# A seventh ring slot, memory keys written feature-major, and table and register loads moved in a decoder step

## What is computed

```python
for i in range(DEPTH):                      # memory of the prompt, both layers
    kv = rmsnorm(mem_prompt, mem_norm[i]) @ w_mem_kv[i]
    mk.append(kv[..., :XA_WIDTH].reshape(B, N_MEM, XA_HEADS, XA_DIM))
    mv.append(kv[..., XA_WIDTH:].reshape(B, N_MEM, XA_HEADS, XA_DIM))
...
h = rmsnorm(x, norm_mix[i])
mix, ns = conv_mixer(...) or retention_mixer(...)
xa = cross_attn(q_x, mem_ks[i], mem_vs[i])  # softmax(q k / 16) v
x = x + jnp.concatenate([mix, xa], axis=-1) @ w_out
x = x + hier_moe(rmsnorm(x, norm_ffn[i]), ...)
```

## Time and profile before

| | us |
|---|---|
| median of three runs | 1340.07 |
| profiled execution, its own time | 1339.78 |
| its span | 1337.9 |
| TensorE matmuls busy | 1204.8 (90%) |
| TensorE weight loads busy (beside matmuls) | 693.8 (52%) |
| VectorE busy | 355.2 (27%) |
| ScalarE busy | 153.9 (12%) |
| GpSimd busy | 11.2 (1%) |
| mean granted TensorE clock | 0.955 |
| bytes moved | 364.59 MB, 273 GB/s in the mean |

### The profile page before, as it was taken

The page is one execution under the profiler, slowest core; times in us unless marked ns, Lnnn a source line. Parts: engine busy times, 40 slices in busy tenths (PEclk is TensorE's granted clock), DMA queues, the critical chain, the costliest instruction groups (busy, mean ns, idle before and its releaser), DMA issues.

```text
span 1337.9 us, 13595 instructions
## 1 busy us (share of the span) xinstructions
PE 1204.8 (90%) x5884; PEld 693.8 (52%) x5884; DVE 355.2 (27%) x868; ACT 153.9 (12%) x340; POOL 11.2 (1%) x22
## 2 busy tenths in 40 slices
PE   6999998998998989869999999996999889888785
PEld 3467776776333434236655555563677743332233
DVE  3222213004021304223234342422300233222224
ACT  2000002002110101010201010110200021000001
POOL 0000000000000000000000000000000000000000
PEclk9999999998999999889999999998999869989998
DMA  9743338731599999994216565557954419999991
GB/s 397 302 159 126 126 128 321 313 126 63 216 430 428 421 428 428 427 427 188 79 63 238 218 227 229 216 240 303 425 188 169 176 34 430 427 428 428 428 426 75
DMA packets 27263, 364.59 MB, mean 273 GB/s; under 512 B 3152, under 2 KB 3168, under 8 KB 5056
## 3 DMA queue, kind: packets, MB, share of 16 engines
q1 hardware_dynamic: 23904, 338.99, 62.1%
q10 hardware_dynamic: 1696, 18.88, 3.4%
q0 software_dynamic: 1600, 5.81, 1.1%
HBM read 339.34 MB, written 24.32 MB: 272 GB/s over the span
## 4 chain that ended last, share of the span: by engine, by line
PE 69%; DMA 26%; DVE 2%; ACT 2%; issue 1%; POOL 0%; SPq 0%; DVEq 0%; POOLq 0%; ACTq 0%
DMA ring<-in_gu 24%; PE bank L621 21%; PE bank L429 12%; PE bank L330 8%; PE bank L486 4%; PE bank L706 4%; PE bank L476 2%; PE bank L517 2%; PE bank L316 1%; PE bank L677 1%; PE bank L442 1%; PE bank L385 1%; PE bank L787 1%; PE bank L408 1%; PE bank L768 1%
## 5 line engine op out<-in xcount | busy, mean ns | idle before, releaser
L621 PE MATMUL bank<-hT,ring 128*128 128x288 f32 x1152 | 285.7, 409 | 4.0 <-DVE hT L1077 3.3
L621 PEld LDWEIGHTS bank<-hT,ring 128*128 128x128 f32 x1152 | 218.8, 191 | 73.7 <-issue 13.9
L486 PE MATMUL bank<-ring,arena 128*32 128x512 f32 x1024 | 132.7, 656 | 55.0 <-DMA ring<-in_gu 53.3
L429 PE MATMUL bank<-arena,ring 128*128 128x288 f32 x640 | 155.7, 406 | 1.8 <-DVEq L1141 1.8
L429 PEld LDWEIGHTS bank<-arena,ring 128*128 128x128 f32 x640 | 121.4, 190 | 35.6 <-issue 2.2
L330 PE MATMUL bank<-ring,arena 128*128 128x512 f32 x256 | 111.2, 594 | 3.1 <-DVE arena L1077 3.1
L486 PEld LDWEIGHTS bank<-ring,arena 128*32 128x32 f32 x1024 | 32.5, 115 | 146.8 <-DMA ring<-in_gu 80.2
L476 PE MATMUL bank<-arena 128*128 128x512 f32 (+1 forms) x192 | 102.0, 659 | 2.4 <-DVE arena L1207 1.7
L330 PEld LDWEIGHTS bank<-ring,arena 128*128 128x128 f32 x256 | 48.2, 190 | 63.4 <-issue 61.9
L517 PE MATMUL bank<-arena 128*128 128x288 f32 x256 | 71.4, 427 | 2.1 <-issue 1.7
L476 PEld LDWEIGHTS bank<-arena 128*128 128x128 f32 (+1 forms) x192 | 32.9, 198 | 73.9 <-issue 72.4
(11 more groups left out here) (206 smaller groups left out, 806.1 us busy)
## 6 DMA issues: line engine op xcount, KB each, us to landing
ring<-in_gu SPq DMA_DIRECT2D x64, 2048.0 KB, 24.9
ring<-in_dn SPq DMA_DIRECT2D x32, 2048.0 KB, 17.4
ring<-in_rin SPq DMA_DIRECT2D x14, 2048.0 KB, 13.4
ring<-in_wkv SPq DMA_DIRECT2D x8, 2048.0 KB, 17.4
ring<-in_cin SPq DMA_DIRECT2D x8, 2048.0 KB, 8.7
ring<-in_kc SPq DMA_DIRECT2D x8, 2048.0 KB, 8.6
ring<-in_vc SPq DMA_DIRECT2D x8, 2048.0 KB, 14.0
ring<-in_st SPq DMA_DIRECT2D x8, 2048.0 KB, 14.9
```

Source lines behind the costliest of these rows:

```text
L429: mm = pe.matmul(bank[1 + o % 4][:, 0:T], w[:, k, :], cat[:, k, :], start=(k == 0), stop=(k == kt - 1))
L486: mm = pe.matmul(bank[2][32 * e:32 * e + 32, :], xt[:, k, 32 * e:32 * e + 32], wv[:, e, kk, :], start=(k == 0), stop=(k == KD - 1), skip_g ...
L621: mm = pe.matmul(outs[o], w[:, o, k, :], src[:, k, :], start=(k == 0), stop=(k == KD - 1))
```

## The change

- `R` goes from 6 to 7. The further passes keep six slots (`SPILL`). The room comes from the descriptor scratch, given as 2,048 bytes of each partition in place of the default, and from the arena, 576 words shorter: `th` and `nrm` (`ms`, `rstd`) move into regions of other stages.
- Key pieces (c < 2) of `memory_kv` are computed with the weight as the stationary side, 128 features x 256 tokens in each half of a bank; ACT copies the banks straight to `KT`, and the key outputs are stored from `KT` and put in order on the host side. `turn_keys`, `keys_turned`, `Ktok`, `keys1` and their waits go. ACT's wait for the store of the layer-0 keys moves from before the first query copy to before layer 1's key copies; VectorE's wait for the store of layer 1's keys goes.
- `squares` issues an activation `Sqrt` of one element before the squares; after the square root of the norms `ffn0` and `ffn1`, and at the start of `attention`, stands an `Exp` of one element.
- TensorE, ACT and VectorE load `npass` before the last pack, GpSimd before its wait for the last pack. The branches stay where they were.

```diff
-R = 6
+R = 7
+SPILL = 6
...
-KEYS_IN = {1: (0, 1), 3: (2, 3)}
...
-        arena = sb("arena", 21568)
+        arena = sb("arena", 20992)
...
-        th = [ar(MSO + 288 * i, T) for i in range(2)]
+        th = [ar(SQO + 1184 + 288 * i, T) for i in range(2)]
...
-        nrm = ar(MSO, 576)
+        idle = small[0:1, 62:63]
+        nrm = ar(PHO + 2752, 576)
...
@@ TensorE, memory_kv
+                if c < 2:
+                    for o in range(2):
+                        f = (2 * mb + o) * P
+                        for k in range(KD):
+                            if i == 0 and j == 0 and o == 0:
+                                pe.wait_ge(S("normed"), k + 1)
+                            mm = pe.matmul(bank[KV_BANKS[i][j]][:, o * NM:(o + 1) * NM], w[:, k, f:f + P],
+                                           src[:, k, :], start=(k == 0), stop=(k == KD - 1), skip_group_check=True)
+                    mm.then_inc(S("kv_sum"), 1)
+                    return
...
@@ TensorE, experts; the same two lines on ACT and VectorE
                 for i in range(PACKS):
+                    if i == PACKS - 1:
+                        pe.wait_ge(S(f"npass{L}"), 1)
+                        more = pe.value_load(npass[0:1, L:L + 1], min_val=0, max_val=PASSES - 1)
...
-                    if L == 0 and i in KEYS_IN:
-                        pe.wait_ge(S("gt_out"), i)
-                        turn_keys(1, KEYS_IN[i])
-                        pe.wait_ge(S("kt_out_a"), 2 + KEYS_IN[i][1] + 1)
...
-            pe.wait_ge(S("ktok_out"), 4)
-            turn_keys(0, range(4))
-
-            pe.wait_ge(S("kt_out_a"), 2)
-            pe.wait_ge(S("kt_out_d"), 2)
+            pe.wait_ge(S("kt_out"), 4)
             pe.wait_ge(S("v_out"), 4)
...
@@ ACT, squares
+                act.activation(idle, C("eps")[0:1, :], ACT.Sqrt)
                 for k in range(KD):
...
                 act.activation(ms[:, 0:n], bank[7][:, 0:n], ACT.Sqrt, scale=1.0 / D, bias=C("eps")) \
                    .then_inc(S("ms_out"), 1)
+                if name in ("ffn0", "ffn1"):
+                    act.activation(idle, C("eps")[0:1, :], ACT.Exp)
...
@@ ACT, keys_ahead
+                act.wait_ge(S("keys_stored0"), 16)
                 for j in range(4):
                     act.wait_ge(S("kv_sum"), 8 + j + 1)
-                    act.activation(keys1[:, j % 2, (j // 2) * 512:(j // 2 + 1) * 512],
-                                   bank[(4, 7, 0, 1)[j]][:, :], ACT.Copy).then_inc(S("kv1_out"), 1)
+                    act.activation(KT[:, 2 * j:2 * j + 2, :], v3(bank[(4, 7, 0, 1)[j]][:, :], 2), ACT.Copy) \
+                       .then_inc(S("kv1_out"), 1)
...
@@ ACT, attention
                 act.wait_ge(S("normed"), NORM_DONE[f"mix{i}"])
+                act.activation(idle, C("eps")[0:1, :], ACT.Exp)
...
-            dve.wait_ge(S("keys_stored1"), 16)
...
-    nc = bacc.Bacc("TRN2", target_bir_lowering=False, num_devices=1)
+    nc = bacc.Bacc("TRN2", target_bir_lowering=False, num_devices=1, dynamic_dma_scratch_size=2048)
```

More of the change, by code:

```diff
@@ L289, in spill @@
                             sp.wait_ge(S(f"spill_dve{L}"), p * (STEP_DVE * PACKS) + i * STEP_DVE + SPILL_DVE["began"])
-                            for j in range(R):
+                            for j in range(SPILL):
                                 src = a["gu"][bass.ds(i * 4 + (L * 4 * PACKS + j), 1)] if j < 4 else \
@@ L332, in memory_kv @@
                 mm.then_inc(S("kv_sum"), 1)
[L334 to L341, removed]
             def attention(i):
@@ L857, in memory_kv @@
                     act.wait_ge(S("kv_sum"), j + 1)
-                    act.activation(Ktok[:, j % 2, (j // 2) * 512:(j // 2 + 1) * 512], bank[j][:, :], ACT.Copy) \
-                       .then_inc(S("ktok_out"), 1)
-                for g in (1, 3):
-                    act.wait_ge(S("kt_turned"), g + 1)
-                    act.activation(KT[:, 2 * g:2 * g + 2, :], v3(bank[g][:, :], 2), ACT.Copy) \
-                       .then_inc(S("kt_out_a"), 1)
+                    act.activation(KT[:, 2 * j:2 * j + 2, :], v3(bank[j][:, :], 2), ACT.Copy).then_inc(S("kt_out"), 1)
             def keys_ahead():
+                act.wait_ge(S("keys_stored0"), 16)
                 for j in range(4):
                     act.wait_ge(S("kv_sum"), 8 + j + 1)
-                    act.activation(keys1[:, j % 2, (j // 2) * 512:(j // 2 + 1) * 512],
-                                   bank[(4, 7, 0, 1)[j]][:, :], ACT.Copy).then_inc(S("kv1_out"), 1)
+                    act.activation(KT[:, 2 * j:2 * j + 2, :], v3(bank[(4, 7, 0, 1)[j]][:, :], 2), ACT.Copy) \
+                       .then_inc(S("kv1_out"), 1)
                 act.wait_ge(S("kv1_out"), 4)
-                act.dma_start(a["out_mk"][1].rearrange("(m p) n -> p m n", p=P), keys1) \
+                act.dma_start(a["out_mk"][1], KT) \
                     .then_inc(S("keys_stored1"), 16)
@@ L894, in store_state @@
                     .then_inc(S(f"state_stored{f}"), 16)
-            def keys_turned(groups):
-                for g in groups:
-                    act.wait_ge(S("kt_turned"), 4 + g + 1)
-                    act.activation(KT[:, 2 * g:2 * g + 2, :], v3(bank[(4, 7)[g % 2]][:, :], 2), ACT.Copy) \
-                       .then_inc(S("kt_out_a"), 1)
             def attention(i):
                 act.wait_ge(S("normed"), NORM_DONE[f"mix{i}"])
+                act.activation(idle, C("eps")[0:1, :], ACT.Exp)
                 for j in range(9):
@@ L954, in experts @@
                 for i in range(PACKS):
+                    if i == PACKS - 1:
+                        act.wait_ge(S(f"npass{L}"), 1)
+                        more = act.value_load(npass[0:1, L:L + 1], min_val=0, max_val=PASSES - 1)
                     act.wait_ge(S("gu_sum"), 4 * PACKS * L + 4 * i + 4)
@@ L960, in experts @@
                         values_ahead(VALUES_IN[i])
-                    if L == 0 and i in KEYS_IN:
-                        keys_turned(KEYS_IN[i])
                     act.wait_ge(S("gt_turned"), PACKS * L + i + 1)
@@ L1085, in memory_kv @@
                        .then_inc(S("v_out"), 1)
-                for g in (0, 2):
-                    dve.wait_ge(S("kt_turned"), g + 1)
-                    dve.tensor_copy(KT[:, 2 * g:2 * g + 2, :], v3(bank[g][:, :], 2)).then_inc(S("kt_out_d"), 1)
             def attention(i, xo):
@@ L1255, in experts @@
                 for i in range(PACKS):
+                    if i == PACKS - 1:
+                        dve.wait_ge(S(f"npass{L}"), 1)
+                        more = dve.value_load(npass[0:1, L:L + 1], min_val=0, max_val=PASSES - 1)
                     dve.wait_ge(S("tanh"), PACKS * L + i + 1)
@@ L1476, in store_memory @@
             def store_memory():
-                pool.wait_ge(S("ktok_out"), 4)
-                pool.dma_start(a["out_mk"][0].rearrange("(m p) n -> p m n", p=P), Ktok).then_inc(S("keys_stored0"), 16)
+                pool.wait_ge(S("kt_out"), 4)
+                pool.dma_start(a["out_mk"][0], KT).then_inc(S("keys_stored0"), 16)
                 pool.wait_ge(S("v_out"), 4)
```

22 lines of the change are left out of this document (5 added, 17 removed).

## The result

The changed kernel takes 1307.41 us (median of four runs, 1302.5 to 1309.8), the kernel before 1340.12 on the same chip (1339.09 to 1340.31): ratio 0.975, 95% interval 0.972 to 0.978. That is 32.7 us less, and 21.6 were forecast; the direction was right, the size lies outside the range. The profiled execution took 1305.89 us with a span of 1304.1, 33.8 under the span before.

A forecast was written before the change was run, and what follows sets the result against it. The prediction took TensorE to set the end, except where it waits for the ring, a quarter of the span. Its terms summed to 21.6 us, taken from the profiled 1339.78 to give 1318.2 us; range 1311 to 1327.

The forecast's parts named there:

- the pass count: Branch after the experts, both layers: loading earlier removes 0.7 us ahead of each branch, 1.4 in all, not the branch itself.
- memory keys: Layer 0: key matmuls write the keys turned, so the projection begins 1.6 us earlier; in layer 1 nothing.
- the square roots: Routing norms of both layers: ACT's table load for the square root leaves the chain, 1.3 us each, 2.6 in all.
- the first softmax: First attention: the exponential begins 1.3 us earlier, plus 0.7 for a dip of TensorE's clock that may go, 2.0 us.
- the routing exponentials: Routing of layer 1: the early table load gains 0.65 us, limited by the ranks, whose last matmul ended at 1081.22.
- seventh slot, two expert stages: Each expert stage has one slot fewer to fetch, as pack 1's first is fetched early: 4.9 us each, 9.8 in all.
- seventh slot, second attention: Second attention: keys 3 are issued together with keys 2, beside the same store, so it ends 3.85 us earlier.
- The small activation at the start: Ahead of the memory's squares, for which TensorE waits: the added one-element activation costs 0.3 us.
- Rival (5): Slower: weight loads of the memory key matmuls don't hide, 48.6 us at the full 190 ns, giving 1366.8 us; chance 0.03.
- Rival (1): The clock falls out otherwise: layer 1's picking matmuls get 4.5 us back after earlier exponentials, giving 1313.7 us; chance 0.20.
- rival (4): Concerns the table loads; its statement and size are cut from the text given; chance 0.03.
- GpSimd's scratch: GpSimd's transfers with the smaller descriptor scratch: cost taken as 0, at most 3.0 us if the second close transfer must wait.

## Why the prediction was wrong

The range failed at one step: **the pass count**, "Loading earlier removes the 0.8 ahead of the branch, not the branch", and in the list of what would show it, "the branch is as long as before". The first half holds as far as it goes (0.73 and 0.41 us against 0.7 each). The second treats 6.12 and 3.63 us as the price of a branch, when it is the price of that branch at that place in TensorE's program. The part called memory keys moved it by 192 instructions, and both branches became short, with a granted clock of 1.00 in place of 0.75 in the norm sum behind the first: 12.0 us, by the kernel before with 192 idle instructions, where nothing else was changed. No rival had it. One row shown ahead of the prediction spoke of it: the same instruction with 6122 and 3626 ns, with nothing in the computation to explain the difference. The prediction set no lower bound to the branch. Had it let both fall to a third of a microsecond, for which no row gave the number, the low end of the range, 1311, would have gone down by another 9 us and held the result. The result without the 12.0 us would be 1319.4, near the forecast, and that nearness is partly luck: the square roots were taken 2.4 us too high and the first softmax 1.0, the routing exponentials 0.9 too low, and the totals carry a microsecond or two that no term has.

Term by term:

| term | forecast | runs |
|---|---|---|
| seventh slot, two expert stages | 9.8 | 5.4 + 4.5 = 9.9 |
| seventh slot, second attention | 3.85 | 3.9 |
| memory keys, with the small activation ahead of them | 1.3 | 1.6 |
| first softmax | 2.0 | 1.0 |
| square roots of two norms | 2.6 | 0.17 |
| routing exponentials, layer 1 | 0.65 | 1.6 |
| loads of the pass count | 1.4 | 1.1 |
| length of the branches | 0 | 12.0 |
| sum | 21.6 | 31.3 |

The sum of the right column is 1.4 us short of the 32.7 measured, well within what single runs differ by.

*The seventh slot* came out as worked, in size and in its signs (pack 1 fetched ahead, one wait in the attention, 4.9 us a slot). What looked like a surplus of 3.2 us in stage 0 of the kernel after is mostly luck of the profile of before. Its windows (columns as the earlier trace rows):

```profile
358.00:362.00 4.00, 3.91 (x24) 1.34 (x28) 0.00 (x0) 0.00 (x0) 0.00 (x0) 0.57 0.26 103
576.00:584.00 8.00, 7.46 (x30) 3.71 (x23) 2.59 (x6) 0.38 (x1) 0.00 (x0) 0.57 1.00 426
...
1078.00:1082.00 4.00, 3.22 (x18) 3.08 (x17) 2.00 (x11) 1.62 (x12) 0.00 (x0) 0.56 0.00 0
```

The first two lie in stage 0 at a granted clock of 0.57, and all seven other kernels with six slots are 2.5 to 3.4 us faster there. Stage 1 goes by its picking matmuls as well, which are drawn by the run. Kernels with seven slots gain 8.0 and 8.6 us there with picks of 7.9 and 8.0 us, and 3.3 to 5.7, the kernel after among them, with picks of 10.5; those with six gain 2.8 to 4.5 with fast picks and -2.5 to 0 with slow ones.

*Memory keys*: no transposes and no second copy, and the size as worked. The sum of the second norm stands ahead of layer 0's last key and value matmuls; first the kernel before, then the kernel after:

```profile
45.63 1.13 PE L316 MATMUL bank<-arena,cst 128*128 128x288 f32 x4
...
45.23 1.13 PE L315 MATMUL bank<-arena,cst 128*128 128x288 f32 x4
```

From there to the projection (76.67 and 74.66) it is 31.0 us in all seven kernels with the old keys and 29.4 in all seven with the new ones: 1.6. The other 0.4 of the 2.01 in the table came ahead of it and are luck: by the run, the clock moves that point by up to 4 us in kernels of either kind (44.98 to 49.10 us in those without idle instructions at the head; granted clock over 17 to 25 us 1.00 in both kernels shown here, 0.57 with the loads alone, at 49.05). The small activation at the start, priced at 0.3, costs at most 0.2: TensorE's first matmul begins at 9.22 to 9.33 us with it, and at 9.10 to 9.29 without. Rival (5), weight loads that don't hide, is refuted by the 218 ns.

*Square roots.* The step "1.3 each" took a load that ended at 304.47 as standing alone between the sum and the root. The sum of squares ended only at 303.12 + 1.24 = 304.36 in that profile, so the load was hidden but for 0.1 us: 0.08 and 0.09 measured. The row of the matmuls beside the load wasn't read:

```profile
303.12 1.24 PE L316 MATMUL bank<-arena,cst 128*128 128x288 f32 x4 [0.99 <-DVE arena L1066]
```

The stretch with the first of these norms is 1.66 us longer in the kernel after. All 13 other profiles are longer there than the one of before, by 0.03 to 1.66, with and without the small activations, so this is no cost of them.

*First softmax*: 1.03 for the load, and the 1.7 us of slow clock go or stay by the run, not by the load: they are missing in kernels without the small activations as well (granted clock over 205 to 230 us: 0.93 before, 1.00 in all 13 other profiles).

*Routing exponentials*: the cap "their last matmul ended at 1081.22" took the ranks' time as fixed. Before, at a granted clock of 0.56 (the third window above), they took 1.47 us; in the kernel after they took 0.83, at 0.96:

```profile
1054.00:1057.00 3.00, 2.19 (x18) 2.08 (x18) 2.46 (x13) 0.00 (x0) 0.00 (x0) 0.96 0.00 0
```

That part is not the tables' alone. Of the six kernels with the small activations three have ranks of 0.83 us, at a granted clock of 1.00 while they run, and gain 2.0 us from the second output projection to the picks; the other three have ranks of 1.41 to 1.47 us, at 0.50 to 0.53, and gain 1.2. The eight without them have -0.4 to 0.8. The difference of the means is 1.7, of which the norm's load is 0.1. Rival (1) expected the picks behind the ranks to profit too. In the kernel after they took 10.54 us, at a granted clock of 0.55, as before (0.56); in five other kernels they took 7.4 to 8.0, at 0.74 to 0.81, and in one 11.5, at 0.50. The three runs of before ahead of the prediction lie within 1.2 us and suggest low stretches that are the same in every run; the forecast left them so. More runs of that kernel lie between 1333 and 1345 us, with mean granted clocks of 0.951 to 0.963, so they differ by the run.

*The table loads themselves*, rival (4): no run shows a cost of a load beyond its own 1.28 us. The small activation of the kernel after starts at 578.95, 1.30 us after its load did, and takes 0.20.

*GpSimd's scratch*: no cost shows. The kernel with the ring alone, which has the small scratch, gains no less than the slots explain (17.7 us, 13.7 expected).

*Why the place matters.* The page of after lists the queue "q8 instruction" with 49 packets and 0.80 MB, 16.3 KB each. The page has 13,779 instructions, and the two instruction queues move 0.91 MB, about 66 bytes each, so one such packet holds an estimated 250 instructions: near the distance after which the lengths seem to repeat. A long branch ends right behind such a packet, and during a short one none is under way. The author's reading, which no run shows, is that a branch is long when what it jumps to lies in a packet that is still to come, and that moving it by a part of a packet changes this. That every long branch ends behind a packet is shown (12 of 12); that this packet holds the branch's target is not, since no view tells what a packet holds. The reading also fits the two lengths of before: with the ring's transfers on the engines the packet started 3.6 us after the first branch, with none beside it 1.0 us after the second. The 2.17 and 2.88 us belong to packets that had started already or started sooner; why they did is open, and no run holds the place and changes the transfers beside it.

## What to carry to other kernels

Before the length of a control instruction is taken as fixed, put idle instructions at a few distances ahead of it, in a stretch that waits anyway: here that alone was worth 13.9 us, as much as the seventh slot. The DMA view over the branch tells whether there is something to gain: a packet of an instruction queue that ends inside it, as in all 12 long ones here. A part is credited with what its stretch shows and not with the difference of two totals, since a change in one place moves the code, and the clock, in others: the memory keys, worth 1.6 us, came with a total some 17 us lower. Where a load or a wait is to be hidden, look for the other work that ends at the same time: it sets what is left to gain, and its own time may move too.

## What was not expected of the hardware

- The same COMPARE_BRANCH over the same skipped code takes 0.32 to 6.47 us on TensorE, by where it lies in the program; moves of 64, 192, 256 and 320 instructions gave 2.17, 0.36, 6.40 and 2.88 us for layer 0.
- A long COMPARE_BRANCH on TensorE ends 1.3 to 1.5 us behind a 16.3 KB packet of the instruction queue, in 12 of 12 cases; during none of the 16 short ones is one under way. Its length is the time to the packet's start plus 2.3 to 2.8 us.
- Waits that never wait cost 108 ns each at the head of TensorE's program (the first matmul begins at 14.76 with 128 of them and at 21.65 with 192), and nothing measurable under the ring's waits or, with 64 of them, under the wait for the first squares.
- Kernels whose totals agree have their low-clock stretches (granted clock 0.50 to 0.57) in different places (17 to 25 us, the first attention, picks of layer 1, the end of stage 0), worth up to 3 us each. One profile beside another shows a term of that size only if more than one kernel has it.
